# Sliding-window attention of a two-layer kernel: values through split fp32r pairs, probabilities normalised before they are turned

## The reference, cut to what matters

```
scores = einsum('bnqhgd,bnkhd->bnhgqk', q, kb) * HEAD_DIM ** -0.5
scores = where(valid, scores + alibi_bias, NEG_INF)          # 128 queries x 256 keys a block
probs  = softmax(concatenate([scores, sink], -1), -1)[..., :-1]
out    = einsum('bnhgqk,bnkhd->bnqhgd', probs, vb)
attn_out = out * silu(attn_gate)
y = concatenate([pool_out, attn_out], -1) @ w_out            # w_out is 1024 x 1024
x = x + rmsnorm(y, norm_post)
```

## Time and profile before

| | us |
|---|---|
| median of 3 executions | 1692.31 |
| lowest and highest | 1691.73 and 1692.43 |
| the profiled execution's own time | 1691.72 |
| its span (first to last instruction) | 1689.9 |

### The profile page before, as it was taken

The page is one execution under the profiler, slowest core; times in us unless marked ns, Lnnn a source line. Parts: engine busy times, 40 slices in busy tenths (PEclk is TensorE's granted clock), DMA queues, the critical chain, the costliest instruction groups (busy, mean ns, idle before and its releaser), DMA issues.

```text
span 1689.9 us, 22509 instructions
## 1 busy us (share of the span) xinstructions
PE 1668.2 (99%) x8729; PEld 1384.4 (82%) x8729; DVE 841.9 (50%) x1626; ACT 560.8 (33%) x1280; POOL 510.5 (30%) x402
## 2 busy tenths in 40 slices
PE   7999999999999999999999999999999999999998
PEld 6778788889888787888888887888887999988886
DVE  5330255335253624568076753838412888855714
ACT  5101456334333002440044200441114777741111
POOL 6125033023333333022211133024314745534310
PEclk9999999999999999999999999999999999999999
DMA  6113022233167332111320223126565525226322
GB/s 207 51 63 112 13 63 71 88 109 106 63 215 276 94 105 86 35 44 52 115 79 20 71 69 106 49 92 224 173 223 150 133 59 136 57 69 219 105 112 100
DMA packets 97002, 178.18 MB, mean 105 GB/s; under 512 B 13912, under 2 KB 33792, under 8 KB 96768
## 3 DMA queue, kind: packets, MB, share of 16 engines
q1 hardware_dynamic: 60992, 95.30, 19.4%
q10 hardware_dynamic: 35904, 81.44, 13.7%
HBM read 121.79 MB, written 54.92 MB: 105 GB/s over the span
## 4 chain that ended last, share of the span: by engine, by line
PE 98%; DVE 1%; ACT 1%; DMA 0%; POOL 0%; issue 0%; POOLq 0%; DVEq 0%
PE ps L1229 24%; PE ps L1143 16%; PE ps L845 14%; PE ps L1079 5%; PE ps L1394 5%; PE ps L1334 5%; PE ps L981 4%; PE ps L1278 4%; PE ps L1364 4%; PE ps L1347 3%; PE ps L899 3%; PE ps L1244 2%; PE ps L1257 2%; PE ps L1033 2%; PE ps L1006 1%; PE ps L878 1%
## 5 line engine op out<-in xcount | busy, mean ns | idle before, releaser
L725 POOL TENSOR_SCALAR w_hi<-w_stage 128x1024 fp32r<-128x1024 f32 (+3 forms) x140 | 126.4, 910 | 960.7 <-PE ps L1229 357.2
L732 POOL TENSOR_TENSOR w_lo<-w_stage,w_hi 128x1024 fp32r<-128x1024 f32 (+3 forms) x140 | 270.5, 1940 | 8.9
L1229 PE MATMUL ps<-h2T_hi,w_hi 128*128 128x512 f32 x384 | 156.1, 407 | 0.3 <-issue 0.3
L1143 PE MATMUL ps<-h2T_hi,w_hi 128*128 128x512 f32 x384 | 154.3, 402 | 0.3 <-issue 0.3
L1229 PE MATMUL ps<-h2T_hi,w_lo 128*128 128x512 f32 x384 | 152.4, 397 | 0.0
L1143 PE MATMUL ps<-h2T_hi,w_lo 128*128 128x512 f32 x384 | 151.5, 395 | 0.0
L1229 PE MATMUL ps<-h2T_lo,w_hi 128*128 128x512 f32 x384 | 151.1, 394 | 0.0
L1143 PE MATMUL ps<-h2T_lo,w_hi 128*128 128x512 f32 x384 | 151.0, 393 | 0.0
L2319 DVE SCALAR_TENSOR_TENSOR rope_swapped<-ps,sin_table_T 32x512 f32<-32x512 f32 x192 | 131.9, 687 | 3.9
L1771 ACT ACTIVATE probs_dil<-probs_dil,dil_stats_out 128x256 f32<-128x256 f32 (+2 forms) x192 | 87.5, 457 | 104.3 <-DVE dil_stats_out L2344 104.3
L2452 DVE TENSOR_REDUCE small<-ps 128x1 f32<-128x1024 f32 x64 | 77.7, 1214 | 54.9 <-PE ps L1334 54.9
(11 more groups left out here) (299 smaller groups left out, 3745.2 us busy)
## 6 DMA issues: line engine op xcount, KB each, us to landing
w_stage<-in_w_in SPq DMA_DIRECT2D x76, 512.0 KB, 3.9
w_stage<-in_w_out SPq DMA_DIRECT2D x16, 512.0 KB, 3.7
gate_scr<-gate_tiles ACTq DMA_DIRECT2D x16, 512.0 KB, 4.3
gates<-gate_scr ACTq DMA_DIRECT2D x32, 256.0 KB, 3.3
v_dil_scr<-values_out SPq DMA_DIRECT2D x24, 256.0 KB, 2.0
dil_scr<-dil_out SPq DMA_DIRECT2D x96, 64.0 KB, 1.6
dil_nums<-dil_scr ACTq DMA_DIRECT2D x24, 256.0 KB, 4.1
v_dil<-v_dil_scr SPq DMA_DIRECT2D x23, 256.0 KB, 3.3
```

Source lines behind the costliest of these rows:

```text
L725: last = nc.gpsimd.tensor_scalar(hi_, raw_, 1.0, 0.0, ALU.mult, ALU.add)
L732: last = nc.gpsimd.tensor_tensor(lo_, raw_, hi_.bitcast(F32), ALU.subtract)
L1143: m = pe.matmul(ps[:, gate_bank(u), :], a[:, s, k, P * m_:P * m_ + P], b[:, k, COLS * n:COLS * n + COLS], start=(k == 0 and j == 0), stop= ...
L1229: m = pe.matmul(bank, a, b, start=(k == 0 and i == 0), stop=(k == KT - 1 and i == 2))
```

## The change: what it does

- Values. `v1` becomes `vS`, which holds for each token the high and the low part of each value head side by side (128 columns of a stationary operand: 64 high, 64 low). ACT writes the high part, DVE the low part, once. The turned probabilities are split too, into `probsT_hi` (ACT, `swa_high`) and `probsT_lo` (DVE, `swa_low`), per block of 128 keys. The values product becomes, for each of two value heads, fp32r matmuls with `vS` as weights and 256 columns of turned probabilities (two heads x 128 queries), high then low, summed in PSUM. The result comes out turned already, with the sum over the high values in rows 0 to 63 and over the low values in rows 64 to 127, so `swa_back` goes.
- The merging of the rows: ACT copies one half into the part of `qT` that is no longer needed (`swa_merge`, twice), DVE adds the other half (`swa_total`, twice), POOL multiplies with the gate (`swa_gate`).
- Normalising: DVE keeps the denominator and reciprocal (`inverse`, now for step i at the end of iteration i), and POOL multiplies the probabilities before they are turned (`swa_norm`, four tensor_scalar of 128x256 per step).
- Order: `swa_high` and `swa_low` of step i-2 stand at the head of iteration i, ahead of the softmax of step i on each engine. POOL's steps are placed by hand: 0 to 6 before panel o0, the others after single chunks of o0 and o1.
- `pool_in` has one buffer instead of two, and its steps in slots (2, 4, 6, 8, 12, 14, 16, 18) instead of (2, 4, 6, 8, 12, 13, 14, 15). The evacuations of the filling move by one iteration or stand ahead of the exponentials.
- The output projection waits for the first two chunks of its panel before its first half, and for all four before its second.

```diff
-    POOL_AT = (2, 4, 6, 8, 12, 13, 14, 15)
+    POOL_AT = (2, 4, 6, 8, 12, 14, 16, 18)
+    SWA_STEPS = ((7,), (8,), (9,), (10, 11), (12,), (), (13,), (14, 15, 16, 17, 18))
...
+        def swa_norm(i):
+            t, hh = divmod(i, HH)
+            nk = P if t == 0 else 2 * P
+            pool.wait_ge(*after("swa_recip", i + 1))
+            for j in range(G):
+                h = G * hh + j
+                last = nc.gpsimd.tensor_scalar(pr[:, i % 2, j, 0:nk], pr[:, i % 2, j, 0:nk], st[:, t % 2, 1, h:h + 1], 0.0,
+                                               ALU.mult, ALU.add)
+            last.then_inc(sem("swa_normed"), 1)
+        def swa_gate(i):
...
+            pool.wait_ge(*after("swa_sum", i + 1))
+            pool.wait_ge(*after("fill_evac", 4 if t < 4 else 12))
+            nc.gpsimd.tensor_tensor(aT[:, hh::2, tk], aT[:, hh::2, tk], qT[:, hh::2, tk], ALU.mult).then_inc(sem("swa_aT"), 1)
+        def swa_step(i):
+            if i < TT * HH:
+                swa_norm(i)
+            if i >= 3:
+                swa_gate(i - 3)
...
+            if p == index["o0"]:
+                for i in range(7):
+                    swa_step(i)
...
+                    if p in (index["o0"], index["o1"]):
+                        for i in SWA_STEPS[4 * (p - index["o0"]) + ci]:
+                            swa_step(i)
...
         def swa_transposes(i):
...
-            pe.wait_ge(*after("swa_exp", G * (i + 1)))
+            pe.wait_ge(*after("swa_normed", i + 1))
...
         def swa_values(i):
...
-            for j in range(G):
-                h = swa_head(G * hh + j)
-                for kb in range(nb):
-                    kt = t - nb + 1 + kb
-                    m = pe.matmul(ps[:, 4, HD * j:HD * j + HD], pT[:, 2 * j + kb, :],
-                                  v1[:, kt, HD * (h // 4):HD * (h // 4) + HD], start=(kb == 0), stop=(kb == nb - 1))
+            pe.wait_ge(*after("swa_lo", swa_blocks(i + 1)))
+            if i >= 2:
+                pe.wait_ge(*after("swa_sum", i - 1))
+            for kv in range(2):
+                ops = [(vS[:, t - nb + 1 + kb, kv].rearrange("p a d -> p (a d)"),
+                        p_[:, G * kb + 2 * kv:G * kb + 2 * kv + 2, :].rearrange("p j q -> p (j q)"))
+                       for kb in range(nb) for p_ in (pTh, pTl)]
+                for x_, (a, b) in enumerate(ops):
+                    m = pe.matmul(ps[:, 4 + i % 2, 2 * P * kv:2 * P * kv + 2 * P], a, b, start=(x_ == 0), stop=(x_ == len(ops) - 1))
-        def swa_back(t):
...
         def pool_in(u):
-            if u >= 2:
-                act.wait_ge(*after("pool_lo", u - 1))
+            if u >= 1:
+                act.wait_ge(*after("pool_lo", u))
...
         for i in range(steps + 4):                       # ACT
+            if 2 <= i < steps + 2:
+                swa_high(i - 2)
+            if i in (2, 4, 6):
+                fill_evac(3 + i // 2)
+            elif i == 7 or 9 <= i <= 12:
+                fill_evac(i if i == 7 else i - 1)
+            if i in POOL_AT:
+                pool_hi(POOL_AT.index(i))
+            if i + 1 in POOL_AT:
+                pool_in(POOL_AT.index(i + 1))
...                                                      # exponentials of step i, as before
+            if 2 <= i < steps + 2:
+                swa_merge(i - 2)
             if i >= 5 and i % 2:
                 attn_hi((i - 5) // 2)
...
+        for i in range(steps + 4):                       # DVE
+            if 2 <= i < steps + 2:
+                swa_low(i - 2)
             if i < steps:
                 softmax_in(i)
-            if 2 <= i < steps + 2:
-                normalise(i - 2)
+            if 3 <= i < steps + 3:
+                swa_total(i - 3)
             if i - 1 in POOL_AT:
                 pool_lo(POOL_AT.index(i - 1))
             if i >= 6 and i % 2 == 0:
                 attn_lo((i - 6) // 2)
-            if i >= 4 and i % 2 == 0:
-                back((i - 4) // 2)
+            if i < steps:
+                inverse(i)
```

More of the change, by code:

```diff
@@ L989, in _ @@
         pe.wait_ge(*after("qkv_evac", 8))
-        pe.wait_ge(*after("v1_evac", 2))
         def keys_of(t):
@@ L1507, in _, with swa_high @@
         steps = TT * HH
[L1509 to L1518, removed]
+        def swa_high(i):
+            for kb in range(swa_blocks(i + 1) - swa_blocks(i)):
+                act.wait_ge(*after("swa_T", swa_blocks(i) + kb + 1))
+                if i >= 1 and kb == 0:
+                    act.wait_ge(*after("swa_valued", i))
+                act.activation(pTh[:, G * kb:G * kb + G, :], ps[:, 2 + kb, :].rearrange("p (j c) -> p j c", c=P),
+                               ACT.Copy).then_inc(sem("swa_hi"), 1)
@@ L1531, in attn_hi @@
+            act.activation(mTh[:, k, COLS * n:COLS * n + COLS], pmR[:], ACT.Copy).then_inc(sem("pool_hi"), 1)
         def attn_hi(t):
-            act.wait_ge(*after("swa_aT", t + 1))
+            act.wait_ge(*after("swa_aT", 2 * t + 2))
             tk = slice(P * t, P * t + P)
@@ L2100, in back, with swa_low @@
-        def back(t):
-            dve.wait_ge(*after("swa_backT", t + 1))
-            dve.wait_ge(*after("fill_evac", 4 if t < 4 else 12))
-            dst = aT[:, :, P * t:P * t + P]
-            nc.vector.tensor_tensor(dst, ps[:, 5, :].rearrange("p (j c) -> p j c", c=P), dst, ALU.mult).then_inc(sem("swa_aT"), 1)
+            nc.vector.reciprocal(st[:, t % 2, 1, hs], st[:, t % 2, 1, hs]).then_inc(sem("swa_recip"), 1)
+        def swa_low(i):
+            for kb in range(swa_blocks(i + 1) - swa_blocks(i)):
+                dve.wait_ge(*after("swa_hi", swa_blocks(i) + kb + 1))
+                js = slice(G * kb, G * kb + G)
+                nc.vector.tensor_tensor(pTl[:, js, :], ps[:, 2 + kb, :].rearrange("p (j c) -> p j c", c=P),
+                                        pTh[:, js, :].bitcast(F32), ALU.subtract).then_inc(sem("swa_lo"), 1)
@@ L2107, in pool_lo, with swa_total @@
+        def swa_total(i):
+            t, hh = divmod(i, HH)
+            tk = slice(P * t, P * t + P)
+            src = ps[:, 4 + i % 2, :].rearrange("p (a x q) -> p a x q", a=2, x=2)
+            dve.wait_ge(*after("swa_merge", 2 * i + 2))
+            for x_, rows in enumerate((slice(0, HD), slice(HD, P))):
+                dst = qT[rows, hh::2, tk]
+                last = nc.vector.tensor_tensor(dst, src[rows, :, x_, :], dst, ALU.add)
+            last.then_inc(sem("swa_sum"), 1)
         def pool_lo(u):
```

114 lines of the change are left out of this document (51 added, 63 removed).

## The result

| | before | after |
|---|---|---|
| median of 4 executions, us | 1692.37 | 1699.49 |
| lowest and highest | 1691.73 and 1692.43 | 1698.50 and 1701.99 |
| ratio of the medians, 95% interval | | 1.0045 (1.0032 to 1.0057) |
| span of the profiled execution | 1689.9 | 1699.9 |
| first scores to the start of the output projection of slot 18 ("the stage") | 129.15 | 136.45 |

A forecast was written before the change was run, and what follows sets the result against it. TensorE was taken to bound the kernel, with a ring through ACT and DVE limiting the gain: 15.0 us less work minus 14.2 of stalls wins 0.8, so 1691.5 us in terms of the median, range 1683 to 1698.

The forecast's parts named there:

- TensorE's sum: TensorE in the sliding attention loop: 29.4 us of values and turning back go, 14.4 come, net 15.0 less.
- the ring: ACT and DVE wait for each other once per slot: lap 6.6 us, 8.8 in odd slots where pool_in waits.
- the walk: Slot-by-slot timing of the loop with these laps: stalls sum to 14.2 us, loop ends at 320.5 against 321.43.
- TensorE's 8.68 is longer than the lap: Slots 8 to 11 run at TensorE's 8.68 us each, so 3.2 us are won by slot 12.
- The two short slots without pool_in (12 and 13) have no stall: Slots 12 and 13, short and without pool_in: TensorE was to have no stall there.
- Chunk 1 ends at 282.3 and chunk 3 at 292.9: POOL's panel o1, waiting for reciprocals between chunks, was to end at 292.9 instead of 284.4.
- Catches in slots 13 and 14: POOL's 2.4 us tensor_tensor was to hold DVE's L2084 in steps 13 (+2.1 us) and 14 (+1.5 us).
- Rival C: Shared DVE and POOL port in slots 12 to 16: three more catches cost 7 us, 1698.5; chance 0.12.
- the two signs: Signs of the port: L2084 at 1 to 2 us in steps 13 and 14; o1's last chunk well after 293.
- POOL has no split under way when the reciprocals: Argument against the port rival: no POOL split runs while DVE computes the reciprocals of steps 12, 14 and 15.
- Rival D: Clock falls to 1.2 GHz after stalls in slots 6 and 14: 11.8 us more, some 5 absorbed; 1698.3, chance 0.04.
- Rivals A and B: A: softer ring, about 7 us more won, 1684.3, chance 0.18. B: no ring, all 15.0 won, 1677.3, chance 0.08.

The follow-up runs named there:

- e9: Changed kernel with throwaway matmuls put into TensorE's waits for the low parts in slots 4, 6, 8, 13 and 14; 1700.93 us.
- e2: Changed kernel with ACT's four exponentials no longer waiting for L2121's sum, only the sink's exponential does; 1694.71 us.
- e6: Changed kernel with only the chunks of panel o1 placed anew, chunk 0 before step 11; 1698.81 us.
- e4: Changed kernel with pool_in behind the exponentials, exponentials not waiting for L2121, and softmax_in ahead of the low parts on DVE; 1685.08 us.
- e7: The best version: changed kernel plus pool_in behind the exponentials, exponentials not waiting for L2121, softmax_in ahead of low parts, o1's chunks earlier, L2121 behind low parts; 1682.13 us.
- e1: Changed kernel with pool_in moved behind the exponentials of its iteration on ACT; 1691.86 us.

## Why the prediction was wrong, point by point

In short: TensorE's sum and the ring were right. What failed is the step by which slots 8 to 11 run at TensorE's own 8.68 us while the ring gains slack. POOL's splits caught L2121 in each of steps 7 to 10, the four slots took 38.8 us instead of 34.7, and no slack was left for the fourth silu behind them.

- "The net is 15.0 us less": right. The eight matmuls of a step's values take 0.96 (chain after, slot 15: `323.75 0.96 PE ps L1079 x8`), no turning back, and 121.9 busy in the best version against 120.0, with 1.9 in values behind waits, which the sum did not have.
- "The ring through ACT and DVE": right in place and nearly in size. Laps of 6.77 and 9.17 for 6.6 and 8.8, stalls in slots 4, 6 and 7 of 1.8, 2.3 and 0.6 for 1.1, 2.9 and 0.7, and none in slot 5, where 0.7 was forecast. Slot 8 starts 48.7 us after the first scores, where the walk had 47.1: 1.6 of the 8.1 us by which the end missed (142.1 against 134.0).
- "TensorE's 8.68 is longer than the lap" in slots 8 to 11: this is the step that failed. By it the ring gained on TensorE there, and 3.2 us were won by slot 12. The walk had set catches of L2084 (now L2121) only in steps 13 and 14. The catches of steps 7 to 10 were left out, since I had looked at POOL's splits where they stand in the kernel before and not where the new norms put them. Together they are 2.12 + 1.60 + 2.17 + 1.67 - 4 x 0.16 = 6.9 us. The catch of step 7 makes the lap into slot 8 11.1 us where 8.8 was walked, and by the values of slot 8 the kernel is 3.7 behind the walk instead of 1.6. The laps from there to slot 12 are 8.19, 9.31, 8.25 and 7.85, 33.6 together against 34.8 of TensorE, so the ring gains little on it. Slot 12 starts 5.5 late. Part of that is TensorE's lower clock, but as e9 shows it would otherwise have been a wait. In e2, where the exponentials don't wait for L2121, these four slots take the 34.8 that were forecast.
- "The two short slots without pool_in (12 and 13) have no stall": failed in slot 13, which waits 1.66. The prediction had weighed the silu's two table loads only against the long slots 8 to 11, but the fourth silu stands in ACT's iteration 12, and the lap there is 7.81 (ACT is busy throughout but for the start of the exponentials). With the waits and matmuls around it this slot takes 7.8 instead of 5.9, 2.0 of the 8.1 us of the miss. It costs so much because the ring has no slack left: in e2 the wait is 0.34.
- "Chunk 1 ends at 282.3 and chunk 3 at 292.9": failed. The gate in the step ahead of chunk 0 of o1 waits for the last silu (2.14 at 280.74), so chunk 0 starts at 281.44, and chunk 3 ends at 301.85. From the first scores that is 113.7 us for 106.3 in the walk. The gate is only part of it: e6, where chunk 0 stands ahead of it, still has the end of chunk 3 at 113.1, since the norm ahead of that chunk waits for the late reciprocal of step 13. The cost in the change is small: 1.10 ahead of the output projection of slot 14, and e6 gains nothing that can be told. In e4 it was the chain.
- Catches in slots 13 and 14: two came, in sum as forecast. pool_lo of slot 13 (2.16 instead of 0.69) took the place of L2121 of step 13, and L2121 of step 14 took 2.22. The first makes the longest lap of these slots, 10.7, and the largest wait of TensorE, 3.32 in slot 14; the second makes the lap behind it 8.8, with a wait of 1.10 in slot 15.
- Rival C, the port, was the one nearest to the result: 1698.5 for 1699.5, and the two signs that I named for it came (catches beyond those walked, o1 ending well after 293). But I looked for it in slots 12 to 16, and had it at 0.12; the further catches are in steps 7 to 10, so that its number comes out is luck. What spoke against it, "POOL has no split under way when the reciprocals" of steps 12, 14 and 15 "are computed", is not true of step 12: its denominator (L2127) takes 0.68 us at 284.62 instead of 0.16, and ends at 285.30 where POOL's L746 ends at 285.28. That costs 0.5 us beside the ring; what matters is L2121.
- Rival D: the clock did fall, behind the waits of slots 4, 8 and 14 (1.76, 2.16 and 3.32 us), of which it had named slot 14; behind slot 6 it did not. It cost nothing net (e9), so that its number, 1698.3, lies near the result is luck as well. It had 11.8 us of slower matmuls, "some 5" of them taken up by the waits; 4.9 were measured, and all of them were. The Trainium skill (TensorE: Matmul & The Clock Gate, Part 1) says that the throttled state is the default and pauses bring it back. My reading of the trace, that stalls up to 4.3 us cost no clock, was wrong on that: the trace now agrees with the page in direction, but not after each pause of that size (below).
- Rivals A and B: refuted for the change as it stands. e7 shows what B would have needed: all three links off the ring, and the panel ahead. It comes to 10.0 of the 15.0; of the rest 1.9 are the values behind waits and 2.8 the waits of slots 13 to 15.

What stays open: the split of the loss over the three links (undoing one changes what another costs: 7.6, 4.8 and 6.4 singly, 14.4 together), and the part that an order without any catch would give, since a catch can't be removed by itself without moving POOL's work.

## What to carry to other kernels

When TensorE loses work to other engines, write down the lap through their in-order queues, one instruction after another, and compare it with the new slot: here 6.6 against 5.89 ate the gain of the short slots, while ACT was busy for only 89 of 142 us. Then walk POOL's new timeline too and lay each long tensor_tensor on DVE's small ones: an instruction of 0.16 us on the ring costs 2 when it is there. And take off the ring what its waiter doesn't need (the sum for the sink, a load's wait). Here a few short edits of the order made the same change 17 us faster.

## What was not expected of the hardware

The clock. The granted clock fell behind some waits of TensorE and not behind others of the same length. In the change (TensorE's timeline, the wait in brackets):

```profile
212.17 0.38 PE L1079 MATMUL ps<-probsT_hi,v_pair 128*128 128x256 f32 x1 [1.76 <-DVE probsT_lo L2135]
213.25 1.91 PE L1063 MATMUL ps<-ident,probs 128*128 128x128 f32 x8
...
228.08 0.39 PE L1079 MATMUL ps<-probsT_hi,v_pair 128*128 128x256 f32 x1 [2.25 <-DVE probsT_lo L2135]
229.15 1.03 PE L1063 MATMUL ps<-ident,probs 128*128 128x128 f32 x8
```

Behind 1.76 us the eight transposes take 1.91, behind 2.25 they take 1.03. The window from 214 to 220 has a granted clock of 0.78, that is partly at 1.2 GHz. It fell behind 2.16 and 3.32 too, but not in e1 behind 2.30. The same wait of slot 6 was 2.25 us in the change and 2.31 in e6; there the clock fell, to 0.50 in the window from 229 to 231. So the length of the wait alone does not tell. The start of the kernel, with 11.1 us idle of 30 and a clock of 1.00, was no ground to say that it does not fall at all.

A wait too short to see. A matmul's record of 0.39 us covers the 0.23 to the next one, so some 0.16 us of each wait shows as busy time. Eight of these, with the slower second matmul behind each, made about 2 us in e7 that no view lists as waiting.
